# Two small buffers go from the top of SBUF into the running allocation, and everything behind them moves by 640 bytes

## What is computed

```
# first block
u = rmsnorm(x) ; proj = u @ w_in
h = x + concat(fourier_mix(proj[:1024]), dilated_attention(q, k, v)) @ w_out
h = h + square(relu(rmsnorm(h) @ w_up)) @ w_down
x = rmsnorm(h)
# second block: x with a context of 256 tokens; six modulation vectors from c @ w_mod
lat, ctx = project_heads(norm(x)), project_heads(norm(ctx))
x = x + gt1 * merge(gla_scan(lat, ctx), mlstm_scan(lat, ctx)) @ w_out_2
x = x + gt2 * conv_ffn(rmsnorm(x) * (1 + sc2) + sh2)      # 3x3 depthwise conv, SwiGLU
return rmsnorm(x, g_final)
```

## Time and profile before

| | us |
|---|---|
| median of 3 runs | 2555.88 |
| lowest, highest | 2553.91, 2559.26 |
| the profiled execution's own time | 2555.88 |
| its span in the profile | 2554.1 |
| TensorE busy | 2470.5 (97% of the span) |
| VectorE busy | 1682.9 (66%) |
| ScalarE busy | 1130.3 (44%) |
| transfers | 531.96 MB, mean 208 GB/s |

### The profile page before, as it was taken

One profiled execution on the slowest core, in us unless ns is written; L12 is line 12 of the kernel. 1 busy time (PEld: TensorE's weight loads), 2 busy tenths in 40 slices (PEclk: granted clock), 3 DMA queues, 4 the chain that ended last, 5 costly groups with the idle time before them and its releaser, 6 DMA issues.

```text
span 2554.1 us, 32066 instructions
## 1 busy us (share of the span) xinstructions
PE 2470.5 (97%) x12476; PEld 2067.4 (81%) x12476; DVE 1682.9 (66%) x2073; ACT 1130.3 (44%) x1368; POOL 0.2 (0%) x4
## 2 busy tenths in 40 slices
PE   8999999999999999999899999889899999999997
PEld 6886788888888888878678888678788888888876
DVE  5434587878877867654258745775688758875775
ACT  5433545435445445554255443234444434443343
POOL 0000000000000000000000000000000000000000
PEclk9999899999999999999999999999999999999999
DMA  7661467777878777545649856015455565555554
GB/s 281 191 196 58 166 238 277 285 286 278 298 266 293 290 282 264 173 160 196 231 158 359 320 192 217 2 58 191 132 189 185 181 208 185 188 190 191 188 154 135
DMA packets 133351, 531.96 MB, mean 208 GB/s; under 512 B 14944, under 2 KB 14944, under 8 KB 121840
## 3 DMA queue, kind: packets, MB, share of 16 engines
q1 hardware_dynamic: 133232, 530.31, 59.8%
HBM read 528.16 MB, written 2.10 MB: 208 GB/s over the span
## 4 chain that ended last, share of the span: by engine, by line
PE 92%; DVE 4%; ACT 1%; issue 1%; DMA 1%; ACTq 0%; SPq 0%; DVEq 0%
PE PSA L673 20%; PE PSA L580 17%; PE PSA L582 17%; PE PSA L581 17%; PE PSA L674 10%; PE PSA L710 2%; PE PSA L677 1%; PE PSA L676 1%; PE PSA L741 1%; PE PSA L753 1%; DVE XX L1869 1%; PE PSA L1033 1%; DVE cv L1560 0%; PE PSA L589 0%; PE PSA L921 0%
## 5 line engine op out<-in xcount | busy, mean ns | idle before, releaser
L1608 DVE TENSOR_TENSOR wlo<-raw,whi 128x1024 fp32r<-128x1024 f32 x788 | 932.9, 1218 | 410.6 <-ACT whi L1142 408.8
L1142 ACT ACTIVATE whi<-raw 128x1024 fp32r<-128x1024 f32 x788 | 800.6, 1053 | 499.5 <-DMA raw<-in_w_down 189.8
L673 PE MATMUL PSA<-u,whi 128*128 128x512 f32 x2250 | 802.5, 399 | 3.8 <-DVE wlo L1608 2.7
L674 PE MATMUL PSA<-u,wlo 128*128 128x256 f32 x2250 | 632.5, 281 | 0.0
L673 PEld LDWEIGHTS PSA<-u,whi 128*128 128x128 f32 x2250 | 423.4, 188 | 102.1 <-DVE wlo L1608 3.0
L674 PEld LDWEIGHTS PSA<-u,wlo 128*128 128x128 f32 x2250 | 425.7, 189 | 7.1
L580 PE MATMUL PSA<-whi,u 128*128 128x512 f32 x1088 | 427.8, 393 | 3.3 <-DVE zl L1969 2.2
L581 PE MATMUL PSA<-wlo,u 128*128 128x512 f32 x1088 | 425.8, 391 | 0.0
L582 PE MATMUL PSA<-whi,u 128*128 128x512 f32 x1088 | 425.6, 391 | 0.0
L580 PE MATMUL PSA<-whi,ahi 128*128 128x512 f32 x856 | 334.0, 390 | 2.8 <-DVE wlo L1608 2.8
L581 PE MATMUL PSA<-wlo,ahi 128*128 128x512 f32 x856 | 333.7, 390 | 0.0
(11 more groups left out here) (279 smaller groups left out, 1628.4 us busy)
## 6 DMA issues: line engine op xcount, KB each, us to landing
raw<-in_w_up SPq DMA_DIRECT2D x300, 512.0 KB, 3.5
raw<-in_w_in SPq DMA_DIRECT2D x208, 512.0 KB, 4.3
raw<-in_w_down SPq DMA_DIRECT2D x192, 512.0 KB, 4.2
mod_slot<-in_w_mod_rows SPq DMA_DIRECT2D x78, 1024.0 KB, 6.4
raw<-in_w_out SPq DMA_DIRECT2D x64, 512.0 KB, 3.8
raw<-in_w_mod SPq DMA_DIRECT2D x36, 512.0 KB, 3.8
raw<-in_w_down2b SPq DMA_DIRECT2D x20, 512.0 KB, 3.7
h<-in_x SPq DMA_DIRECT2D x2, 1024.0 KB, 6.5
```

The costliest lines, as they stand in the source:

```text
L673: pe.matmul(both, wh[:, c], u_pair[:, k, :], start=k == 0, stop=False)
L674: mm = pe.matmul(main, wl[:, c], uhi[:, k, :], start=False, stop=False)
L1142: AF(whi[:, n % SLOTS, 0:w], raw[:, n % SLOTS, 0:w], ACT.Copy).then_inc(hi_done, 1)
L1608: TT(wlo[:, n % SLOTS, 0:w], raw[:, n % SLOTS, 0:w], whi[:, n % SLOTS, 0:w], ALU.subtract).then_inc(lo_done, 1)
```

## The change

`colA` and `astat` are allocated in the running order, `colA` before `stat` and `astat` behind `part`, and no longer at the top. The limit of `z_at` goes up by the 640 bytes that are free there now.

```
         modT = at("modT", [P, NMODCH, 2], F32)
+        colA = at("colA", [P, 6, KD], F32)
         stat = at("stat", [P, 8, 4], F32)
         part = at("part", [P, TC, 4], F32)
+        astat = at("astat", [P, NH, 8], F32)
         bgate = at("bgate", [P, 16], F32)
         levels = at("levels", [P, 2 * LEVELS * P], U8)
         cst = at("cst", [P, 64], F32)
         modrow = at("modrow", [P, UW], F32)
         Z = cur[0]
         K = 1024
-        colA = at("colA", [P, 6, KD], F32, 229344 - 640)
-        astat = at("astat", [P, NH, 8], F32, 229344 - 256)
         diag0 = at("diag0", [P, TC, P], F32, Z - 1024)
...
-            assert Z + off + size <= 229344 - 640, (name, Z + off + size - 229344)
+            assert Z + off + size <= 229344, (name, Z + off + size - 229344)
```

## The result

The changed kernel takes 2572.58 us (2571.97 to 2573.9, 4 runs) against 2555.81 us of the kernel before beside it (2553.91 to 2559.26): ratio 1.0073, 95% interval 1.005 to 1.0095. It is 17 us slower, and the forecast of no change was wrong. The four times alone give 1.0066; the record has four more executions of the changed kernel, 2571.68 to 2585.06 us.

What follows compares the result with a forecast made beforehand. The prediction took TensorE's matmuls, busy 2470.5 of 2554.1 us, as the bound. All terms were 0, so the 2554.1 us span plus 1.8 us around it gave 2555.9 us, range 2552 to 2560.5 us.

Steps and rivals of the forecast that it cites:

- What bounds the kernel: Whole kernel: number of TensorE matmuls times their pace, plus short chains of small instructions; TensorE busy 2470.5 of 2554.1 us.
- Stationary tiles in the moved region: 2568 dn-phase matmuls reading `ahi`/`alo`: no change of duration from the new address, term 0, bounds 0.8 us either way.
- The pace follows none of the three: Three token-phase stretches: 224.4 to 224.7 ns per matmul whatever the transfer share, VectorE's load or the stationary buffer.
- Slower rival: dn phases: stationary and moving operands at different remainders lengthen every matmul by 3 ns, 7.7 us, giving 2563.6 us; chance 0.07.
- Elementwise work: Convolution taps and ScalarE's `CN` writes in the moved region: no effect of the address, term 0, bound 1.0 us either way.
- Readers of `colA`: ScalarE activations: the extra 91 ns is the second operand, not the place; term 0, bounds 1.5 us less, 0.6 us more.
- Transfers: Loads into the moved region, mostly `mod_slot`: landing perhaps 3% shorter by the skill's rule, nothing waits; term 0, bounds 0.
- Faster rival: Small instructions on 204 us of the chain: operands at multiples of 256 served 3% faster, 6.1 us, giving 2549.8 us; chance 0.05.
- `colA` rival: Norm 2 transposes: the place of `colA` costs the 91 ns after all, at most 1.5 us saved, 2554.4 us; chance 0.04.

Runs made afterwards that it cites:

- e5: The changed kernel with 128 unused bytes ahead of `Z`, so `Z` is 128 past a multiple of 256 again: 2557.67 us, ratio 0.9991 to the kernel before.
- e1: The kernel before with only `colA` moved into the running order, `astat` left at the top: 2572.32 us, ratio 1.0052.
- e3: The kernel before with the whole allocation begun 128 bytes later, only `colA` and `astat` staying: 2558.41 us, ratio 0.9993.
- e2: The kernel before with only `astat` moved into the running order, `colA` left at the top: 2556.33 us, ratio 0.9995.
- e7: The kernel before with `stat` allocated ahead of `raw`, so `whi` and `u` start 128 bytes later and `Z` stays: 2572.44 us, ratio 1.005.
- e8: The kernel before with `stat` allocated between `whi` and `u`, so `u` moves to 128 past them modulo 256: 2566.94 us, ratio 1.0029.
- e4: Matmuls alone, no model computed, start addresses of both operands swept in steps of 64 bytes: 226.9 to 227.9 ns per matmul at distance 0, 232.4 at 128.
- e6: Matmuls alone, no model computed, operand distance swept from 0 to 240 in steps of 16: 226.7 ns per matmul at 0, 233.3 at 128.
- e9: Matmuls alone, no model computed, up and dn patterns by operand distance: up pairs 353.2 ns at 0, 347.1 at 240; dn 226.7 at 0, 232.5 at 128.
- e10: The kernel before with `u` begun 16 bytes later and `bgate` at the top, `Z` unmoved: 2558.76 us, ratio 1.0003.
- e13: Matmuls alone, no model computed, dn and up patterns behind breaks of short matmuls: dn at distance 16 took 234.0 to 234.8 ns, at 0 227.9 to 228.6.
- e12: The kernel before with `u` 32 bytes later only for the two norms that feed up phases, `bgate` at the top: 2543.76 us, ratio 0.9947.
- e11: The changed kernel with `u` begun 16 bytes later and 64 unused bytes ahead of `Z`: 2555.3 us, ratio 0.9992 to the kernel before.

## Why the prediction was wrong, point by point

*What bounds the kernel*: right in the main. 15.7 of the 17.6 us are the dn phases' matmuls at a slower pace, and TensorE's idle sum did not grow; the rest is a balance of other stages, above all of the granted clock in the context states.

*"Stationary tiles in the moved region. Term: 0. Bounds: ... 0.8 us either way"*: this step failed: the term that was put at 0 measured 15.7 us. Three faults made the zero and its bound. The three stretches of rows 4 differ in load, traffic and buffer, but all have distance 0; "The pace follows none of the three" was true and said nothing of an address. The bound of 0.3 ns was finer than the count can show: one matmul more or less in 156 is 1.4 ns, and by the starts the pace is 226.7 ns and not 224.4. And the rows taken for the remainder, `wsh` in rows 6 and the loads in rows 5, are durations of the weight load, which stays at 188 ns in both kernels; the cost sits between the starts of the matmuls. A test of the remainder in a duration that does not carry the cost is no bound.

*Slower rival: "stationary and moving operand at different remainders"*: the right condition, and its sign came: 396 ns in the dn phases alone, in and up phases as before. With 0.07 it had too little weight, and it was too cheap: it was priced at 3 ns for 2568 matmuls, 7.7 us, and is 6.6 ns in most of them, 15.7 us. How the distance slows a matmul no run shows. "Against it: ... the stationary operand begins 128 and 640 past already" was a wrong argument: 512 apart is the same modulo 256, by which it goes. Where the trace has no row at another distance, "not seen" should have stood as no bound above, and a range up to such a price.

*Elementwise work*: right. `CN` 386 to 388 ns, the taps' median 415 ns as before.

*Readers of `colA`*: right. 564 ns with `colA`, 474 with `vec` as before, though `colA` now lies at a multiple of 64. So the 91 ns are not the place; e5 shows both new places to be free.

*Transfers*: the zero on the path stands. The rule that the prediction quotes from the Trainium skill, "DMA: Bandwidth & Descriptors", section "How a descriptor splits into AXI transactions", is neither borne out nor refuted for the SBUF side. The estimate by it, 3%, is 0.2 us of 6 us, less than equal placements differ: medians to landing of `mod_slot` are 6.1, 6.2 and 6.0 us at a multiple of 256 (changed kernel, e1, e3), and 6.4, 5.9, 6.6, 5.9 and 5.9 us at 128 past one (before, e2, e5, e7, e8). The row of the changed kernel:

```profile
DMA to landing us min/median/max: 4.7/6.1/10.3
```

*Faster rival, `colA` rival*: fell with rows 6 to 8 unchanged.

## What to carry to other kernels

When an allocation moves, ask for every pair of matmul operands that stream together whether their distance modulo 256 bytes changes, and weigh the answer by the number of such matmuls: 6.6 ns looks like nothing and was 0.6% here. Read a pace from the starts of consecutive matmuls, not from durations, and do not take a row as evidence on an address unless that address really varies in it. A sweep can miss a second pace: at distance 16, e4, e6 and e9 had only the fast pace and e10 and e13 the slow one. A few bytes of shift, chosen per phase, can also be a gain: e12 is 0.5% faster than the tuned kernel with no instruction more.

## What was not expected of the hardware

The pace of 512-column float32r matmuls with a new 128 x 128 stationary tile each depends on the distance of the two operands' start addresses modulo 256: in e6 226.7 ns at 0, 232 to 234 at 32 to 160, 229.0 at 192, 233 at 208 and 224, 227.0 at 240. Four bytes are enough: e6 has 232.5 ns at 4, 230.8 at 8 and 233.3 at 252. Why it repeats by 256, and why the best distance is 0 for one pattern and near 112 or 240 for that of 512 and 256 columns, was not tried, nor was another type or shape. The placement has no effect on the weight load's own duration, 188 ns in both kernels.

One source of the spread of equal kernels showed by the way. The stretch of the heads between `inL` and `out2` took 157.2 us in the kernel before and 163.9 in e7, 169.2 in e11, with the same instructions. The rows of these three, columns as in rows 3, give mean granted clocks of 0.97, 0.89 and 0.88, so more of the stretch ran at the lower level of 1.2 GHz; ahead of it TensorE had been busy throughout `inL` in all three (235.6 of 235.6 us, the same, and 234.7 of 234.9). What makes the difference is not shown.

```profile
1563.80:1721.00 157.20, 136.88 (x862) 112.95 (x860) 116.38 (x222) 60.95 (x113) 0.00 (x0) 0.97 0.20 73
```

```profile
1572.10:1736.00 163.90, 147.66 (x862) 122.04 (x860) 116.62 (x222) 60.94 (x113) 0.00 (x0) 0.89 0.20 70
```

```profile
1560.10:1729.20 169.10, 151.51 (x860) 122.94 (x859) 116.49 (x222) 60.78 (x113) 0.00 (x0) 0.88 0.19 68
```
